# Seven block products in place of eight for the second product of the last perceptron, groups 0 to 2

## The reference

```python
def sqrelu_mlp(h, w1, w2):
    a = jax.nn.relu(h @ w1)
    return (a * a) @ w2
```

## Time and profile before

| | |
|---|---|
| time, median of 3 runs | 2926.14 us (2922.74 to 2926.99) |
| span of the profiled execution | 2926.7 us |
| TensorE matmuls busy | 2837.7 us (97%) |
| VectorE busy | 1374.1 us (47%) |
| ScalarE busy | 1144.5 us (39%) |
| GpSimd busy | 1320.1 us (45%) |
| mean granted TensorE clock | 0.991 |

### The profile page before, as it was taken

How to read it: one execution, slowest core, us unless ns; L and a number is a source line. 1 busy time by engine, 2 the same in 40 slices (tenths; PEclk the granted TensorE clock), 3 DMA queues, 4 the chain that set the end, 5 groups by cost and what they waited for, 6 DMA issues and landing times.

```text
span 2926.7 us, 41107 instructions
## 1 busy us (share of the span) xinstructions
PE 2837.7 (97%) x16278; PEld 2342.1 (80%) x16278; DVE 1374.1 (47%) x2568; ACT 1144.5 (39%) x1955; POOL 1320.1 (45%) x851
## 2 busy tenths in 40 slices
PE   7789999999999999989999999999999999999999
PEld 7577778888888786778888787888878878888887
DVE  4448653141121476632111467776543468667432
ACT  4353554453332443543322444332433543323332
POOL 4253247874444441344444553344534633435344
PEclk9999999999999999999999999999999999999999
DMA  6834114553223324032333332111222421212223
GB/s 242 318 113 142 51 44 146 180 165 100 94 94 130 110 82 156 1 108 87 96 99 94 111 113 70 58 58 58 87 72 87 137 88 47 66 58 73 87 72 115
DMA packets 84862, 300.69 MB, mean 103 GB/s; under 512 B 9536, under 2 KB 9920, under 8 KB 84288
## 3 DMA queue, kind: packets, MB, share of 16 engines
q1 hardware_dynamic: 84672, 298.07, 31.5%
HBM read 295.94 MB, written 2.10 MB: 102 GB/s over the span
## 4 chain that ended last, share of the span: by engine, by line
PE 84%; DVE 10%; ACT 2%; issue 2%; DMA 1%; POOL 1%; SPq 0%; POOLq 0%; ACTq 0%; DVEq 0%
PE ps L639 65%; PE ps L612 5%; DVE ps L2438 4%; PE ps L814 3%; PE ps L835 2%; PE ps L667 1%; PE ps L1011 1%; PE ps L1074 1%; PE ps L1085 1%; PE ps L939 1%; DMA t<-in_wmod 1%; PE ps L1252 1%; DVE t L2738 1%; DVE t L2776 1%; PE ps L952 0%
## 5 line engine op out<-in xcount | busy, mean ns | idle before, releaser
L639 PE MATMUL ps<-t,t 128*128 128x512 f32 (+3 forms) x9936 | 2218.6, 381 | 22.0 <-DVE t L2140 7.3
L639 PEld LDWEIGHTS ps<-t,t 128*128 128x128 f32 x9936 | 1781.0, 189 | 368.7 <-issue 35.5
L3087 POOL TENSOR_TENSOR t<-t,t 128x1024 fp32r<-128x1024 f32 (+3 forms) x464 | 1082.3, 2337 | 1078.8 <-ACT t L1397 1040.3
L1397 ACT ACTIVATE t<-t 128x1024 fp32r<-128x1024 f32 (+3 forms) x464 | 476.5, 1031 | 840.8 <-PE ps L639 784.9
L612 PE MATMUL ps<-t,t 128*128 128x128 f32 (+2 forms) x1662 | 238.4, 278 | 25.8 <-DVE t L2347 3.9
L612 PEld LDWEIGHTS ps<-t,t 128*128 128x128 f32 (+2 forms) x1662 | 190.1, 141 | 72.8 <-ACT t L1546 16.6
L2541 DVE TENSOR_TENSOR ps<-ps,t 128x512 f32<-128x512 f32 (+1 forms) x96 | 57.3, 606 | 343.7 <-ACT t L1739 343.7
L2558 DVE TENSOR_TENSOR t<-ps,t 128x512 f32<-128x512 f32 x56 | 38.2, 692 | 201.0 <-PE ps L639 200.9
L2438 DVE SCALAR_TENSOR_TENSOR ps<-t,t,ps 128x512 f32<-128x512 f32 (+1 forms) x174 | 116.1, 667 | 6.4 <-ACT ps L1654 0.6
L3107 POOL TENSOR_TENSOR t<-t,t 128x4 f32<-128x4 f32 (+2 forms) x96 | 86.4, 900 | 59.8 <-DVE t L2144 27.4
L814 PE MATMUL ps<-t,t 96*128 96x384 f32 (+1 forms) x320 | 104.6, 449 | 4.8 <-DVE t L2301 2.4
(11 more groups left out here) (279 smaller groups left out, 2480.3 us busy)
## 6 DMA issues: line engine op xcount, KB each, us to landing
t<-in_wbig SPq DMA_DIRECT2D x424, 512.0 KB, 3.5
t<-in_wmod SPq DMA_DIRECT2D x96, 512.0 KB, 6.6
t<-in_wbig SPq DMA_DIRECT2D x16, 416.0 KB, 3.1
t<-in_wbig SPq DMA_DIRECT2D x16, 332.0 KB, 2.9
t<-in_wbig SPq DMA_DIRECT2D x14, 256.0 KB, 2.6
t<-in_wbig SPq DMA_DIRECT2D x6, 384.0 KB, 3.1
t<-in_x SPq DMA_DIRECT2D x1, 2048.0 KB, 7.7
out<-t SPq DMA_DIRECT2D x8, 256.0 KB, 4.4
```

The source lines that it names most:

```text
L639: m = p.matmul(out, lhs, rhs, start=kk == 0 and n == 0, stop=kk == tiles - 1 and n == 2)
L1397: a.activation(c.hi(w), c.raw(w), ACT.Copy).then_inc(w_hi.h, w_hi.up(("cut", w)))
L3087: g.tensor_tensor(c.lo(w), c.raw(w), c.hi(w).bitcast(F32), ALU.subtract).then_inc(w_lo.h, w_lo.up(("cut", w)))
```

## The change

In groups 0 to 2 of `ml1` the second product (512 tokens x 1024 hidden columns, times 1024 x 1024 weights) is made by Winograd's form of Strassen's method. The activations A and the weights B are cut into 2 x 2 blocks. Seven block products take the place of eight: 11, T3, 21, T4, T1, T2, 22, in this order. Group 3 and all else stay as they were.

- Each product is 256 tokens x 512 hidden columns x 512 output columns, from two "units" r of 128 x 1024 weights, 12 matmuls each: 24 matmuls a product, 168 a group.
- The squares no longer stay in PSUM: relu goes to SBUF (L1871, tiles `HF`), VectorE squares there (L2723, first input in PSUM).
- VectorE makes four sums of activation blocks a group (`full`, L2737: parts T3, T1, T2, 22) and eight sums of weights (`summed`, L2750, L2756, L2761: weights T3, T2, T1, T4, each for r 0 and 1), all in place in SBUF, 128 x 1024 elements each.
- The seven activation parts are cut into high (ScalarE, L1884) and low (VectorE, `low`, L2728), 128 x 1024 each.
- The 14 weight units of a group are cut as before: high by ScalarE (L1490), low by GpSimd (L3337; `by_vector` returns False for all).
- VectorE takes a product out of two banks at once (`took`, L2775 and L2778, 128 x 2 x 512): nine a group in place of eight instructions of 128 x 512.
- The raw weights of the seven products come in eight DMAs a group into buffers of their own (`fetch_part`), a group ahead from group 1 on.
- The row of the residual (`row_of`) is made after group 2 in place of group 0.

```diff
+WN = ("11", "T3", "21", "T4", "T1", "T2", "22")
+WN_ONTO = {"T4": "T3", "T2": "11", "22": "T1"}
+def seven(n, g):
+    return n == "ml1" and g < 3
+def by_vector(x):
+    return False
...
         # pe_program, mlp
+            for name in WN:
+                at, onto = pairs[WN_PAIR[name]], WN_ONTO.get(name)
+                if onto:
+                    P.wait_ge(dve, ("took", n, g, onto))
...
+                P.wait_ge(act, ("parth", n, g, name))
+                P.wait_ge(dve, ("partl", n, g, name))
+                for r in range(2):
...
+                    P.wait_ge(w_hi, ("cut", x))
+                    P.wait_ge(dve if by_vector(x) else w_lo, ("cut", x))
+                    for k in range(2):
+                        for b in range(2):
+                            for m_, (wp, ap) in enumerate(((hi, aH), (hi, aL), (lo, aH))):
+                                m = p.matmul(c.BK[at + b], ...
...
         # act_program, cut
+            if isinstance(w, tuple):
+                if w[3][0] == "T":
+                    A.wait_ge(dve, ("sum", w))
+                else:
+                    A.wait_ge(c.s_wn[w[3:5]], ("raw", w))
+                a.activation(c.hi(w), c.wn_from(w), ACT.Copy).then_inc(w_hi.h, w_hi.up(("cut", w)))
...
         # dve_program, mlp
+        def low(g, name):
+            V.wait_ge(act, ("parth", n, g, name))
+            v.tensor_tensor(lo, c.wn_full(n, name), hi.bitcast(F32), ALU.subtract)...
+        def full(g, name):
+            V.wait_ge(dve, dve.n)
+            out, one, other, op = {"T3": (A12, A11, A21, ALU.subtract), "T1": (A21, A21, A22, ALU.add),
+                                   "T2": (A11, A21, A11, ALU.subtract), "22": (A12, A12, A11, ALU.subtract)}[name]
+            v.tensor_tensor(out, one, other, op)...
+        def summed(g, name, r):
...
+            else:
+                key, onto = {"T1": ("22", "T3"), "T4": ("21", "21")}[name]
+                V.wait_ge(dve, ("sum", ("wn", n, g, "T2", r)))
+                V.wait_ge(w_lo, ("cut", ("wn", n, g, onto, r)))
+                m = v.tensor_tensor(raw(WN_FROM[name]), raw(key), raw("sum"), ALU.subtract)
...
         # pool_program, cut
+            if isinstance(w, tuple):
+                if not by_vector(w):
+                    G.wait_ge(w_hi, ("cut", w))
+                    g.tensor_tensor(c.lo(w), c.wn_from(w), c.hi(w).bitcast(F32), ALU.subtract)...
+                continue
```

More of the change, by code:

```diff
@@ L317, in direct @@
     def direct(self, u):
-        return self.units[u][0][0] in ("wq", "wkv", "pw")
+        return not isinstance(u, tuple) and self.units[u][0][0] in ("wq", "wkv", "pw")
     def use(self, item):
@@ L998, in mlp, with freed @@
         for g in range(4):
             for h in range(2):
[L1000 to L1003, removed]
-            if g == 0:
+                def freed(b):
+                    return ((dve, ("hf" if seven(n, g) else "bl", n, g, 4 * h + b)),)
@@ L1005, in mlp @@
+                yield from product_gemm(("w1", n, g, h), "FM", (c.AH, c.AL), T, 512, 8, prepared(n), freed,
+                                        banks=[q + m for q in pairs[2 * h:2 * h + 2] for m in range(2)])
+            if seven(n, g):
+                yield from seven_products(g)
+            else:
+                yield from weave(down(g), ahead, rate) if g == 3 and rate else down(g)
+            if g == (2 if n == "ml1" else 0):
                 row_of(n, i, 1, int(n[1] == "c"))
@@ L1762, in mlp, with first_parts, seven_products @@
+        def first_parts(g):
+            yield
+            for name in ("11", "T3"):
+                part(g, name)
+                yield
+        def seven_products(g):
+            at = {0: "21", 2: "T4", 4: "T1", 6: "T2", 9: "22"}
+            for m, x in enumerate(("wn", n, g, name, r) for name in WN for r in range(2)):
+                cut(x)
+                if m in at:
+                    part(g, at[m])
+                yield
+                yield
         for g in range(4):
             for h in range(2):
-                main = product_gemm(("w1", n, g, h), 4, 8, lambda b: relu(g, h, b))
+                main = product_gemm(("w1", n, g, h), 4, 8, lambda b: (positive if seven(n, g) else relu)(g, h, b))
+                if seven(n, g) and h:
+                    main = weave(main, first_parts(g), 0.25)
@@ new lines, in first_parts, with seven_products @@
+        def first_parts(g):
+            yield
+            full(g, "T3")
+            yield
+            low(g, "11")
+            yield
+            low(g, "T3")
+            for name in ("T3", "T2"):
+                for r in range(2):
+                    yield
+                    summed(g, name, r)
+        def seven_products(g):
+            yield
+            low(g, "21")
+            full(g, "T1")
+            yield
+            took(g, "11")
+            full(g, "T2")
+            summed(g, "T1", 0)
+            yield
+            summed(g, "T4", 0)
+            took(g, "T3")
+            yield
+            summed(g, "T4", 1)
+            low(g, "T4")
+            yield
+            summed(g, "T1", 1)
+            took(g, "21")
+            yield
+            low(g, "T1")
+            full(g, "22")
+            yield
+            took(g, "T4")
+            low(g, "T2")
+            yield
+            took(g, "T1")
+            low(g, "22")
+            yield
+            took(g, "T2")
+            took(g, "22")
@@ L3292, in mlp @@
                 yield from product_gemm(("w1", n, gr, h), 4, 8, lambda b: None)
-            yield from weave(down(gr), chain((0,), ahead), rate) if gr == 3 and rate else down(gr)
+            if seven(n, gr):
+                for name in WN:
+                    for r in range(2):
+                        cut(("wn", n, gr, name, r))
+                        yield
+                        yield
+            else:
+                yield from weave(down(gr), chain((0,), ahead), rate) if gr == 3 and rate else down(gr)
     def bc(col):
```

176 lines of the change are left out of this document (161 added, 15 removed).

## The result

| | before | with the change |
|---|---|---|
| time, median of 4 runs | 2926.41 us (2922.74 to 2926.99) | 2942.36 us (2936.05 to 2943.64) |
| span of the profiled execution | 2926.7 us | 2939.8 us |
| TensorE matmuls | 16278 | 16206 |

The changed kernel is slower by about half a per cent: the ratio is 1.0054, with a 95% interval of 1.0039 to 1.0068. The forecast was 2940.0 us in a range of 2929 to 2951. The matmuls did go, 16278 - 16206 = 72.

A forecast was written before the change was run, and what follows sets the result against it. TensorE bounds the kernel before; with the change VectorE and GpSimd together bound the second product. 2926.7 + 12.9 (16.3 saved already contained) + 1.0 for the clock = 2940.6, as median 2940.0 us; range 2929 to 2951.

The forecast's parts named there:

- The matmuls removed: On TensorE, 24 matmuls fewer a group, 72 in all at 0.2267 us: 16.3 us off; second product 38.1 us for 43.5.
- The turns: In the second product, VectorE's two-SBUF-input instructions and GpSimd's cuts run one after the other: 46.5 us against TensorE's 38.1.
- D: Price of one VectorE instruction with two SBUF inputs behind a GpSimd cut: 1.1 us.
- P: Price of one GpSimd cut behind a VectorE instruction: 2.3 us.
- GpSimd is not held up: Rival: only VectorE waits, GpSimd's 33.5 us of cuts fit into 38.1; 2909.8 up to 2916 us; chance 0.10.
- The walk: Step-by-step second product of one group: largest stall 5.3 us before T4, 47.8 us in all, +12.9 us over three groups.
- The clock: After the stall TensorE may run one stretch at 1.2 GHz, 1.9 us more, mostly hidden in waits: 0.3 us a group, +1.
- At nothing: Items put at no cost: `full`, `took`, ScalarE's additional copies, first banks of the next `w1`, DMAs, moving `row_of`.
- The half rival: VectorE's instructions fall into GpSimd's gaps, T4's chain costs 2 us: second product 42 to 44 us, 2921 to 2931; chance 0.07.

The follow-up runs named there:

- e1: The changed kernel with GpSimd's cuts of the seven products' weights made on 16 of 1024 columns: 2913.01 us, beside 2925.32 of the kernel before.
- e10: e9 with all 14 cuts made by GpSimd, VectorE's other instructions in the same order: 2936.74 us.
- e2: The changed kernel with VectorE's block sums T1, T2, 22 and weight sums T1, T4 on 16 of 1024 columns: 2922.29 us.
- e4: The changed kernel with 24 matmuls nobody reads added before TensorE's waits for T4: 2940.83 us, ratio 1.0052 to the kernel before.
- e6: e5 with the residual's row moved into group 3 and the third bank exchange dropped: 2930.12 us against 2924.92 of the kernel before, ratio 1.0020.
- e8: e6 with T1 ahead of T4, the row inside group 3's first half of `w1`, VectorE's order rewritten: 2930.31 us, ratio 1.0018 to the kernel before.
- e9: e8 with four of 14 cuts by VectorE in place of seven, full T2 and 22 earlier: 2930.58 us, ratio 1.0020 to the kernel before.
- e5: The changed kernel with each product's second unit cut by VectorE, low T4 and T4's sums earlier as in e3: 2936.51 us against 2924.92 before.
- e3: The changed kernel with low T4 and T4's sums ahead of full T2 and T1's sums on VectorE: 2940.46 us, ratio 1.0049 to the kernel before.

## Why the prediction was right

- **The matmuls removed (-16.3 us).** Right, and shown by e1: 168 matmuls take 38.24 us where 38.1 were forecast. An estimate by the 215.8 ns of the Trainium skill (TensorE: Matmul & The Clock Gate, "Wait — 56ns, not 53.3ns?") is 168 x 0.2158 = 36.3; the trace decides for 38.
- **The turns, D = 1.1 and P = 2.3 us.** Right in their sum, 3.4 us forecast and 3.34 in e10; the two were not measured apart. The rule in the Trainium skill, SBUF — State Buffer, "SBUF: two separate sides" (a lock for a whole instruction, not a shared bandwidth), agrees with e10, where VectorE's SBUF instructions and the cuts run one after the other, 3.34 us a pair, and e1 and e2 go the same way: with either partner's instructions made short the second product falls from 48.1 to 38.1 and 40.9 us. The rival "GpSimd is not held up" was wrong: its cuts took 3027 ns in the mean and not 2390.
- **The walk.** T4's first matmul was put 23.1 us behind the end of `w1` and came at 1469.31 - 1445.91 = 23.4; the stall was 5.98 in place of 5.3 us; the product took 47.8 to 48.2 us against 47.8. The small wait at 21 fell before its second unit (0.34 us) and not its first. A group lasts 1493.99 - 1402.39 = 91.6 us, as the 91.5 forecast. In sum +13.6 us, against 12.9 and 1.0 for the clock. Part of this closeness is luck, since the steps in between were off and made up for one another. The sum for T2, put to end at 2.6 us, ended at 5.3, one turn later, and low 21 at 8.7 in place of 6.0. That was made up because GpSimd began its four cuts 0.8 us earlier than in the walk, and because VectorE's instructions from `full` for T2 on had hardly a cut to wait for until ScalarE had made T4's high part.
- **The clock (+1 us).** Right in sum, more happened inside: one stretch behind the stall cost 24.84 - 21.8 = 3.1 us a group, 2.7 of them in T4, not 1.9, and took up both waits at T1 and T2, forecast at 2.8 us, where "most of its cost" was to fall. The 0.3 us left over agree with the forecast; that close an agreement is luck, since the stretch was mis-sized by more. e4 shows that the low clock costs next to nothing beyond those waits (47.90 against 48.08 us).
- **At nothing.** Wrong in two places. By the trace the change costs 15.9 us where 13.9 were forecast, and the two waits, 2.3 us, are what is missing. (That the median is 2942.36 - 2940.0 = 2.4 us above the forecast agrees with this but can't show it: the four runs lie between 2936.05 and 2943.64.) Moving `row_of` was put down as "same price elsewhere". But behind group 2 it needs banks that the last `took` has to empty first: 1.32 us. And the banks of the next `w1` were checked for groups 1 and 2 but not `w2` of group 3, where the banks that `pairs` gives to the second half of `w1` are among those that `w2` takes first, so that it waits for that half's low parts (L2681): 1.0 us. ScalarE's copies and the DMAs did cost nothing that the trace shows.
- **The half rival** (42 to 44 us for the product, 2921 to 2931) did not come in the changed kernel. e6, e8 and e9, built later with fewer cuts on GpSimd, come near it at 2930.1 to 2930.6. Its upper end doesn't fit its own condition: 44 us a product would be 2926.1 + 3 x 0.5 = 2927.6 and not 2931.

The expectations that missed (e5, e6, e8, e9, e10 from above, and e3's time) have one thing in common: they sum the shared access as if it were the only limit. The sum is a lower bound: it gave 45.4 us for e10, and the order at T4 and the low clock brought it to 48.66. Half of the cuts on VectorE make that sum small, and then VectorE's own time and the order through ScalarE bind next (e6, e9). What share of the 44.7 us each has is not settled.

## What to carry to other kernels

Fewer matmuls are worth their price only as long as the engines that prepare the operands have room for the additional sums. Before such an exchange, add up the instructions with two SBUF operands on VectorE together with GpSimd's own, as one engine with the durations that the trace shows for them in turns, and hold that against TensorE's time for the stretch, not for the whole kernel. Take the result as a lower bound: the order of the engines comes on top (e9, e10). When a stage is bound so, moving a wait (e3) or removing the low clock behind it (e4) gives next to nothing back. When the order of the work's end is moved, follow the banks and rows into the next part too.

## What the runs showed of the hardware

- When both engines always have work, VectorE's 128x1024 instruction on SBUF operands and GpSimd's cut alternate strictly, 3.34 us a pair over five pairs (e10). Instructions of VectorE that read PSUM fit between without costing a turn (1.21 us each).
- GpSimd's cut of 16 columns in place of 1024 takes 0.22 us when VectorE has no SBUF instruction under way and up to 1.30 us when it has (e1). The mean of 750 ns in the profile's groups is mostly waiting, which the profile counts as busy, as it does in the 3.3 to 3.4 us of VectorE's instructions.
- Within the second product, the half clock came after gaps of 5.98, 3.96, 3.50 and 2.82 us (the changed kernel, e10, e9, e3: granted clock 0.63 to 0.68 in the mean of the 8 us behind, in group 1) and not after those of 2.14 and 1.50 us (e5, e8: 1.00).
